# RWKV stage of a diffusion trunk: projection passes between the inverse's steps put in 16 places a turn rather than 19, and two pairs of PSUM banks exchanged

## The reference

```python
def _wkv_bidir(r, w, k, v, kk, a, s0):
    fwd_bwd = lambda u: jnp.stack([u, jnp.flip(u, axis=1)])
    per_dir = lambda u: jnp.stack([u[0], jnp.flip(u[1], axis=1)])
    seqs = (fwd_bwd(r), per_dir(w), per_dir(k), fwd_bwd(v), fwd_bwd(kk), per_dir(a))

    def step(S, inp):
        r_t, w_t, k_t, v_t, kk_t, a_t = inp
        s_kk = jnp.einsum('...vk,...k->...v', S, kk_t)
        S = (S * w_t[..., None, :] - s_kk[..., :, None] * (kk_t * a_t)[..., None, :]
             + v_t[..., :, None] * k_t[..., None, :])
        return S, jnp.einsum('...vk,...k->...v', S, r_t)
```

## Time and profile before

| | |
|---|---|
| median of 3 runs | 3821.11 us (3817.45 to 3824.01) |
| profiled execution | 3823.22 us, span 3821.4 us |
| mean granted clock | 0.962 of full speed |
| PE busy | 3483.0 us (91%) |
| DVE, ACT, POOL busy | 1575.6, 1047.0, 675.0 us |
| DMA queue of SyncE | 463.87 MB, 33.1% of 16 engines' span |

### The profile page before, as it was taken

The page is one execution under the profiler, slowest core; times in us unless marked ns, Lnnn a source line. Parts: engine busy times, 40 slices in busy tenths (PEclk is TensorE's granted clock), DMA queues, the critical chain, the costliest instruction groups (busy, mean ns, idle before and its releaser), DMA issues. The chain is left out here.

```text
span 3821.4 us, 92862 instructions
## 1 busy us (share of the span) xinstructions
PE 3483.0 (91%) x41864; PEld 1987.9 (52%) x41864; DVE 1575.6 (41%) x2844; ACT 1047.0 (27%) x1829; POOL 675.0 (18%) x583
## 2 busy tenths in 40 slices
PE   7999999999999969989999698998999998789997
PEld 3454445545666655443332345656666666674333
DVE  3574703546667652120000356813266766321111
ACT  2211004304555441021111321104155555211001
POOL 0141201303334330010000002103033333100000
PEclk8999999999999989989999699999999999999998
DMA  5104523431101010349998211833300110067996
GB/s 197 66 1 139 181 66 89 162 94 32 30 22 28 19 47 24 122 159 421 406 392 347 89 55 56 261 102 78 107 24 22 33 30 28 25 238 324 424 424 275
DMA packets 238877, 538.58 MB, mean 141 GB/s; under 512 B 49264, under 2 KB 157056, under 8 KB 205584
## 3 DMA queue, kind: packets, MB, share of 16 engines
q1 hardware_dynamic: 219424, 463.87, 33.1%
q0 software_dynamic: 19056, 68.69, 5.1%
HBM read 514.64 MB, written 17.87 MB: 139 GB/s over the span
## 5 line engine op out<-in xcount | busy, mean ns | idle before, releaser
L1259 PE MATMUL banks<-sb_h,sb_ring 128*128 128x512 f32 (+1 forms) x1344 | 474.7, 512 | 10.5 <-DMA sb_ring<-w_branch 6.9
L1754 PEld LDWEIGHTS banks<-inv 64*64 64x64 f32 x15104 | 303.2, 139 | 188.2 <-issue 185.9
L1754 PE MATMUL banks<-inv 64*64 64x64 f32 x15104 | 340.4, 225 | 51.1 <-issue 17.1
L1259 PEld LDWEIGHTS banks<-sb_h,sb_ring 128*128 128x128 f32 x1344 | 254.4, 190 | 223.9 <-issue 196.6
L1763 PE MATMUL banks<-sb_h,sb_ring 128*128 128x512 f32 (+1 forms) x672 | 327.8, 595 | 7.2 <-DMA sb_ring<-w_in 4.1
L780 PE MATMUL banks<-sb_h,sb_ring 128*128 128x512 f32 x512 | 232.4, 612 | 19.4 <-SPq L244 19.4
L780 PEld LDWEIGHTS banks<-sb_h,sb_ring 128*128 128x128 f32 x512 | 99.9, 197 | 139.2 <-issue 118.5
L3039 PE MATMUL banks<-gu,xs 128*64 128x512 f32 x768 | 168.6, 594 | 2.7 <-DMA gu<-gu_pairs 2.2
L1259 PE MATMUL banks<-sb_branch,sb_ring 128*128 128x512 f32 (+1 forms) x512 | 170.9, 487 | 0.0
L3189 DVE TENSOR_TENSOR hrow<-hrow,banks 128x256 f32<-128x256 f32 x36 | 15.1, 421 | 375.3 <-ACT hrow L3223 375.3
L2439 DVE COPY inv<-banks 128x512 f32<-128x512 f32 x144 | 98.7, 691 | 171.3 <-PE banks L1754 170.4
(11 more groups left out here) (419 smaller groups left out, 5657.7 us busy)
## 6 DMA issues: line engine op xcount, KB each, us to landing
gu<-gu_pairs SPq DMA_DIRECT2D x64, 1536.0 KB, 16.7
gu<-gu_tiles SPq DMA_DIRECT2D x57, 1024.0 KB, 8.7
sb_ring<-w_in SPq DMA_DIRECT2D x24, 2048.0 KB, 9.4
sb_ring<-gu_tiles SPq DMA_DIRECT2D x39, 1024.0 KB, 9.2
vtok<-w_mod POOLq DMA_DIRECT2D x64, 512.0 KB, 5.5
sb_ring<-down_pairs SPq DMA_DIRECT2D x32, 1024.0 KB, 14.0
sb_ring<-w_in SPq DMA_DIRECT2D x26, 1024.0 KB, 5.3
sb_ring<-down_tiles SPq DMA_DIRECT2D x25, 1024.0 KB, 8.3
```

Of the source, the lines that this page charges most:

```text
L1259: mm = nc.tensor.matmul(out, left(kt), right(kt), start=kt == 0, stop=kt == KT - 1)
L1754: m = mm(k.bank[bank][H[to], at:at + w], left, right, start=start, stop=True, skip_group_check=True)
```

## The change

Five things change, all in `rwkv_heads`.

- Three places in `mix` lose their one pass: behind inverse step 1, behind the products with the values (`gram_times_v`), and between inverse steps 5 and 6.
- Three places that had one pass get two: the middle of `chunk_products`, and the two places in `crossing` ahead of `step` 3 and `step` 4. The projections therefore end later: that of keys with the first pass behind inverse step 6 (before: behind step 4), that of values with the first pair of the crossing (before: at the end of the chunk products).
- The banks of the turned values and of the first turned keys are exchanged, and those of the second keys and of the left operand follow. So the value turns no longer use bank 5, and the wait for the raw rows of values (`hold(s.rawin, kept)`) moves from ahead of `value_turns` to ahead of the first `key_turns`.
- The two parts of the first grams change places, since their banks come free in the other order.
- ScalarE copies the raw keys out (`keep(1)`) behind `inverse_norm` and no longer ahead of its part of `gram_times_v`.

```diff
-        V_BANKS, KEY_BANKS, LEFT_BANKS, BONUS_BANK = (1, 5), ((2, 6), (1, 5)), (2, 6), 3
+        V_BANKS, KEY_BANKS, LEFT_BANKS, BONUS_BANK = (2, 6), ((1, 5), (2, 6)), (1, 5), 3
...
                 for c in range(NC):
                     if c == 4:
-                        filler(1)
+                        filler(2)
...
                     filler(2)
                     step(b, 2)
                 if c:
-                    hold(s.rawin, kept)
                     value_turns(c)
                 if b:
-                    filler(1)
+                    filler(2)
                     step(b, 3)
                     for pos in range(1, 4):
                         for z in range(2):
                             across(z, pos)
                 if c:
+                    hold(s.rawin, kept)
                     key_turns(c, 0)
                 if b:
-                    filler(1)
+                    filler(2)
                     step(b, 4)
...
-                    gram_pair(c, 0, 0, [(s.tok, c(8, 5)), (s.tok, c(8, 6))])
+                    gram_pair(c, 0, 1, [(s.tok, c(8, 5)), (s.tok, c(8, 6))])
...
-                    gram_pair(c, 0, 1, [(s.tok, c(8, 7)), (s.tok, c(8, 8))], s.gdone)
+                    gram_pair(c, 0, 0, [(s.tok, c(8, 7)), (s.tok, c(8, 8))], s.gdone)
...
                 inverse(b, 1, filler, 2)
-                filler(1)
                 if c:
                     hold(s.low_in, c(32, 32))
...
                 gram_times_v(b)
-                filler(1)
                 inverse(b, 5)
-                filler(1)
                 inverse(b, 6)
                 filler(2)
...
-                if project:
-                    keep(1, c, b(3, 7))
                 gram_times_v(b)
                 inverse(b, 5)
                 if c:
                     inverse_norm(c)
+                if project:
+                    keep(1, c, b(3, 7))
```

## The result

The changed kernel took 3836.2 us (median of 7 runs, 3833.5 to 3840.4) against 3821.8 us before (7 runs, 3817.5 to 3825.6). The ratio is 1.0037, with a 95% interval of 1.0027 to 1.0047: slower by 14 us. The profiled execution has a span of 3835.7 us. The ratios leave out slow executions; the one here, of the kernel with the banks alone, took 4571.6 us at a granted clock of 0.738.

What follows compares the result with a forecast made beforehand. The matmul engine, busy 97% or more, was taken to bound each turn. Six layer 0 turns at +1.2 us and six layer 1 turns at +0.6 gave +10.8 on the 3821.1 median: 3832, range 3820 to 3845.

Steps and rivals of the forecast that it cites:

- What a pass costs: A projection pass alone takes 1.05 us; the second of a pair adds 0.86, so three added passes cost 2.58 a turn.
- Place A: Behind inverse step 1, ahead of the first decay and rate products: removing the pass gains 0.44 us in layer 0, 0.68 in layer 1.
- Place B: Between the products with the values and inverse step 5: nothing is exposed, so removing the pass gains 1.05 us.
- Place C: Between inverse steps 5 and 6: without the pass the matmul engine waits 0.97 us for a VectorE copy; gain 0.16.
- What is late next: Layer 0, after step 6: GpSimd masks delay VectorE; gain 1.69 us where the inverse is applied, 1.4 at the second-half chunk products.
- rival 1: Layer 0's L2439 copy falls behind the fourth mask, so removals gain nothing there: +21 us, 3842; chance 0.14.
- the sum of the waits foreseen: Layer 1's turn: 2.58 us added, 1.89 gained, 0.2 lost before the variance; net +0.9 before any issue-wait relief.
- the issue waits may shrink, I take 0.3: Layer 1: issue waits, about 1 us a turn, give back 0.3 when the matmul engine stands still elsewhere; net +0.6.
- Rival 3: Evacuations behind inverse steps 1 and 5 are ready when products end, so removed passes were surplus: -6.8 us, 3814; chance 0.08.
- Rival 4: The order isn't as stated, for instance the moved ScalarE copy holds up step 7: adds 7 us, 3839; chance 0.04.
- rival 2: Layer 0's shorter wait at the application and layer 1's issue waits give the cost back: 3819 to 3825, no difference; chance 0.20.
- Edits at nothing: Bank exchange, moved ScalarE copy and later key weight loads: no loop waits; first-crossing value-turn wait goes, key wait grows equally.

Runs made afterwards that it cites:

- the second profile: The changed kernel run and profiled once more, unchanged: ratio 1.0039 (1.0027 to 1.0051) to the kernel before; loop turns 448.1 us in layer 0, 407.5 in layer 1.

## Why the prediction was right

The sign, the size (3832 forecast, 3836.2 measured, a rise of 10.8 forecast and 14.3 measured) and the main reason held: C's pass had covered a wait, and the added passes cover nothing. That the size came so close is in part luck. The loops of the two profiles differ by 19.1 us (17.6 with the second profile), and part of the cost is that of the banks, which the forecast put at about 1 us. By its steps, in layer 0:

- *What a pass costs.* 0.86 for the second of a pair: the table's turns confirm it three times over, and the changed turn falls back by 0.85, 0.86 and 0.86 at its three pairs. Nothing was covered there.
- *Place A.* 0.44 forecast, 0.45 measured alone. In the changed kernel's own turn it is 0.19, with 0.26 of issue wait in step 2. The wait for ScalarE's copy that the forecast wanted in every turn (0.6 us in layer 0, 0.4 in layer 1) shows in three turns of layer 0 (0.27 to 0.48) and one of layer 1 (0.19).
- *Place B.* 1.05 forecast; 0.96 reach the application when it is alone.
- *Place C.* A wait of 0.97 forecast, 1.03 to 1.06 measured, and a gain of 0 for 0.16. The forecast took the 0.14 us from copy to matmul from the application, where the `hold` for the copy is the last; at step 6 one more stands behind it, and it is 0.30.
- *What is late next.* Forecast was a gain of 1.69 at the application and 1.4 at the second half of the chunk products, with waits of 1.2 and 0.3. Measured are 1.42 and 1.12, with 0.61 and 0.18. The copy did get ahead of the last mask, so rival 1 is out. Net 1.45 a turn against 1.2; the 0.25 that are missing are those of place A, with which GpSimd's masks move (they start 0.19 us earlier in the turn). C's 0.16 is not missed here, since the masks and not step 6 set the application. The forecast took the masks as 1.46 us each; in the trace they take 1.27 and 1.72 by turns.

In layer 1 the sum of the waits foreseen was about right: without the issue waits the six turns are 5.2 us longer (4.7 in the second profile), for 6 x 0.9 = 5.4 forecast. The variance waits 0.23 us in three of the six turns (0.2 forecast for each). One term had the wrong sign. The term "the issue waits may shrink, I take 0.3" is the step that failed: they grew, from 10.1 to 12.4 us in layer 1's loop and from 5.0 to 8.1 in layer 0's. At place A it can be seen in the first profile. Without the pass, step 2 runs into an issue wait, and of the 0.68 us forecast 0.15 are left (the second decay products start 16.45 us behind the bonus product, 16.60 before):

```profile
3094.65 0.79 PE L1754 MATMUL banks<-inv 64*64 64x64 f32 x35
3095.98 0.69 PE L1754 MATMUL banks<-inv 64*64 64x64 f32 x29 [0.54 <-issue]
3096.59 1.13 PE L1763 MATMUL banks<-sb_h,sb_ring 128*128 128x512 f32 x2
...
3099.80 0.69 PE L1772 MATMUL banks<-sb_ring 64*128 64x512 f32 x1
```

The same wait (0.4 to 1.0 us) stands there in four of layer 1's six turns. In the second profile this turn has no wait there, and its second decay products start 15.93 us behind the bonus product: the 0.67 us are there in full. So what the change does to the issue waits at one place is not settled by one profile. Their sum was larger in both profiles of the changed kernel (20.5 and 22.3 us, for 15.1), but kernels with the matmul program of before had 14.4 and 19.2. With 5.4 us more of issue waits in place of the 1.8 less, the forecast would have been a rise of 18 us; the loop turns of the two profiles differ by 19.1, and the rest of the program by -4.8. The Trainium skill ("Runtime: NRT & Kernel Launch", section "Instruction fetch mechanics") calls the crossing of an instruction block mostly hidden. The trace agrees as far as that: 183 blocks landed in the loops before, and 27 issue waits stand in them. What is not hidden is 15 us before and 20 after.

Rival 3 (the passes were surplus) is refuted by the wait at C. Rival 4 is too: the moved ScalarE copy held up nothing, and step 7's copy came in time. Of rival 2 one half happened, the shorter wait at the application, and it was taken back behind it. Under *Edits at nothing* the forecast had the bank exchange cost nothing beyond the variance; alone it costs 0.15% (0.05 to 0.25), 2 to 10 us. What stays open: why, and what decides the place and length of an issue wait.

## What to carry to other kernels

A pass between two dependent steps is paid once if it fills the time of an evacuation, and twice if it is moved to where the engine has no wait: count for each place the wait that the pass covers, not the switches saved (0.19 us each here, against 1.05 exposed). Read "issue" waits of a dense stage as a cost of their own that any reordering shifts, and compare turns without one before drawing a conclusion from a total. Effects of 5 us from moving one pass can be theirs alone. And where a wait is on the critical path, look at what stands between the release and the first matmul: a second `hold` that was satisfied long ago still took 0.15 us here, and the price of one place could not be taken over to the other.

## What was not expected of the hardware

- Issue waits of the matmul engine ended 1.4 us (median) behind the landing of a 16 KB packet of the instruction queue. They come to 15 us of the 838 us of the loops before and 20 after.
- 64 semaphore increments in a row on the matmul engine took 9.6 us, 0.15 us each. A semaphore wait that was already satisfied took the same 0.15 us behind another one (step 6: 0.30 us from copy to matmul, 0.15 where the wait for the copy is the last).
- A VectorE operation with two SBUF inputs that began while a GpSimd mask ran took 1.37 to 1.53 us against 0.68 alone, and ended 0.55 us behind the mask's end. A mask that began while such an operation was still under way took 1.72 us, the others 1.27. Where the VectorE operation began first (1003.43 in the changed kernel) it took 0.75 us.
